# Moving convolution sums, recurrence tails and the maxima's split in a two-block network kernel

## The reference, cut to what matters

```python
def mlstm_chunkwise(q, k, v, ig, lf, state):
    ...
        inter = b + m[..., None]
        m_t = jnp.maximum(inter, jnp.max(logw, axis=-1))
        w_inter = jnp.exp(inter - m_t)
        s = jnp.einsum('bhtd,bhsd->bhts', qc, kc) * jnp.exp(logw - m_t[..., None])
        num = jnp.einsum('bhts,bhsd->bhtd', s, vc) + w_inter[..., None] * jnp.einsum('bhvk,bhtk->bhtv', C, qc)
        den = jnp.sum(s, axis=-1) + w_inter * jnp.einsum('bhk,bhtk->bht', n, qc)
        h = num / jnp.maximum(jnp.abs(den), jnp.exp(-m_t))[..., None]
...
def conv_mixer(z, w, b, ln_w, ln_b, rows):
    a = z[..., :W_C] * jax.nn.sigmoid(z[..., W_C:])
    ...
    return jax.nn.silu(layer_norm(a, ln_w, ln_b))
...
def s5_mixer(...):
    ...
        sl = s5_scan(bul.at[:, 0].add(a_bar * h0), a_bar)
    ...
        y = jnp.real(jnp.einsum('gpn,btgn->btgp', c_mat, states)) + d_mat * u
        y = jax.nn.gelu(y.reshape(u.shape[0], u.shape[1], W_D))
        return (y * jax.nn.sigmoid(y @ glu_w.astype(jnp.float32) + glu_b.astype(jnp.float32))).astype(dtype)
```

## Time and profile before

| | us |
|---|---|
| median of 3 runs (2582.73 to 2586.81) | 2583.0 |
| profiled execution | 2585.3 |
| its span | 2583.5 |
| TensorE matmuls busy | 2358.6 (91%) |
| TensorE weight loads busy | 1758.6 (68%) |
| DVE busy | 1269.9 (49%) |
| ACT busy | 769.0 (30%) |

### The profile page before, as it was taken

One profiled execution on the slowest core, in us unless ns is written; L12 is line 12 of the kernel. 1 busy time (PEld: TensorE's weight loads), 2 busy tenths in 40 slices (PEclk: granted clock), 3 DMA queues, 4 the chain that ended last, 5 costly groups with the idle time before them and its releaser, 6 DMA issues. The chain is left out here.

```text
span 2583.5 us, 26237 instructions
## 1 busy us (share of the span) xinstructions
PE 2358.6 (91%) x10746; PEld 1758.6 (68%) x10746; DVE 1269.9 (49%) x1870; ACT 769.0 (30%) x1173; POOL 141.2 (5%) x128
## 2 busy tenths in 40 slices
PE   7999897878899999999999899978797998886999
PEld 3444663667688878788878588955577876443787
DVE  3769628275554334344433464147554385553410
ACT  3100122413333322244322432334352331343310
POOL 0000000200000000000000000045100000011000
PEclk9999899659999999999999999989898998898999
DMA  7440028005233333234333221000202111001332
GB/s 251 156 129 25 1 66 334 1 1 163 74 98 97 94 97 101 80 94 131 94 94 98 74 58 42 17 1 33 78 25 82 42 41 65 5 14 46 106 98 57
DMA packets 272911, 204.15 MB, mean 79 GB/s; under 512 B 17650, under 2 KB 252458, under 8 KB 271864
## 3 DMA queue, kind: packets, MB, share of 16 engines
q1 hardware_dynamic: 257772, 186.31, 23.7%
q0 software_dynamic: 3136, 10.25, 1.1%
q10 hardware_dynamic: 11884, 5.91, 0.8%
HBM read 175.26 MB, written 26.01 MB: 78 GB/s over the span
## 5 line engine op out<-in xcount | busy, mean ns | idle before, releaser
L1919 PE MATMUL bk_in<-h_part,w_part 128*128 128x512 f32 x2112 | 485.0, 392 | 9.5 <-DVE h_part L2207 6.7
L1919 PEld LDWEIGHTS bk_in<-h_part,w_part 128*128 128x128 f32 x2112 | 398.3, 189 | 95.5 <-DVE h_part L2207 7.1
L2005 ACT ACTIVATE w_part<-w_raw 128x1024 fp32r<-128x1024 f32 (+1 forms) x136 | 154.4, 1136 | 549.4 <-PE bk_in L1919 315.9
L2142 DVE TENSOR_TENSOR w_part<-w_raw,w_part 128x1024 fp32r<-128x1024 f32 (+1 forms) x136 | 179.2, 1318 | 226.9 <-ACT w_part L2005 226.8
L1919 PE MATMUL bk_out<-hid_part,w_part 128*128 128x512 f32 x1056 | 244.5, 394 | 7.6 <-DVE hid_part L2218 7.6
L1919 PEld LDWEIGHTS bk_out<-hid_part,w_part 128*128 128x128 f32 x1056 | 201.0, 190 | 51.0 <-DVE hid_part L2218 8.4
L3618 PE MATMUL fo_ps<-fo_hi,fo_part 128*128 128x512 f32 x512 | 161.8, 395 | 21.0 <-DVE fo_part L2366 21.0
L985 PE MATMUL fr_ps<-arena,work 128*128 128x512 f32 x384 | 168.5, 600 | 5.1 <-DMA work<-in_w_in 5.1
L2479 PE MATMUL bk_in<-h_part,sj_part 128*128 128x512 f32 x576 | 135.4, 396 | 6.8 <-DVE h_part L2230 5.7
L985 PEld LDWEIGHTS fr_ps<-arena,work 128*128 128x128 f32 x384 | 73.5, 193 | 96.4 <-issue 91.2
L2889 PE MATMUL aj_ps<-h_part,aj_part 128*128 128x512 f32 x576 | 137.8, 400 | 0.0
(11 more groups left out here) (558 smaller groups left out, 3344.7 us busy)
## 6 DMA issues: line engine op xcount, KB each, us to landing
w_raw<-in_w_ffn_in SPq DMA_DIRECT2D x88, 512.0 KB, 3.8
work<-in_w_mod SPq DMA_DIRECT2D x24, 1024.0 KB, 8.0
w_raw<-in_w_ffn_out SPq DMA_DIRECT2D x32, 704.0 KB, 4.6
work<-in_w_in SPq DMA_DIRECT2D x25, 512.0 KB, 3.8
w_raw<-in_w_in SPq DMA_DIRECT2D x20, 512.0 KB, 3.8
w_raw<-in_w_out SPq DMA_DIRECT2D x16, 512.0 KB, 4.1
work<-in_w_out SPq DMA_DIRECT2D x8, 1024.0 KB, 6.9
kept_mix<-work SPq DMA_DIRECT2D x12, 512.0 KB, 2.6
```

The lines of the kernel that those rows point to most:

```text
L1919: mm = pe.matmul(bank, w_part[:, n % 2, a, k, :], moving(b, k), start=(first and k == 0 and j == 0), stop=(last and k == kt - 1 and j == 2))
L2005: nc.scalar.activation(w_part[:, n % 2, 0, 0:kt, :], w_raw[:, n % 2, 0:kt, :], ACT.Copy)\
L2142: nc.vector.tensor_tensor(w_part[:, n % 2, 1, 0:kt, :], w_raw[:, n % 2, 0:kt, :], f32(w_part[:, n % 2, 0, 0:kt, :]), ALU.subtract).then_in ...
```

## The change

In the front, `turn_inputs` comes before tile 6, `conv_sums` after job 6 and `conv_squares` after job 11; ACT takes the squares after job 9, the roots after job 12 and the gating root after job 14. The matrix `Km` (before: `K`) is brought back from HBM by SP at the end of this stage.

In the recurrence, `inputs(n + 4)` comes ahead of `modulation(n)`; modulations 14 and 15 stand behind `outputs(0)` and `outputs(1)`, and the last row turn behind the transposes, which go into four banks of `pv`. The coefficients `ca` are loaded before piece 11. DVE clears a region of 8 x 512 columns, and ACT and DVE split the maxima there, on 8 partitions; the other 120 stay zero.

In the matrix memory, `rows` contracts over all 128 partitions of this region. ACT multiplies `pE` by `w_in` (`inter`, 8 pieces of 65 columns with a scale for each partition), between its squares and roots; `norm` runs later, and the last `divide` before `gated(0)`. Buffers of the recurrence move to other addresses.

```diff
@@ -490,19 +490,16 @@
   order = [NT, NT + 1] + list(range(NT))
-  m_part = rounded(nc, S, "m_part", X0, 2, 2, T)
-  pick = rounded(nc, S, "pick8", X0 + 4 * T, 8)
+  m_part, pick = S.first_half[:, 0], S.first_half[:, 1, 0, 0:8]
   sq = A.view(X0 + 4 * T + 16, 8, HD)
...
   rs = A.view(X0 + 5 * T + 16, NT // 2, 8)
-  f32 = lambda v: v.bitcast(F32)
-
   def heads(r):
...
   with memory(S) as ctx:
-    s = semaphores(nc, S, ctx, "ml", "kt ktc vs st stc m_hi m_lo pick rows dd m0 m1 scores w ahead states intra inter sum dve"
+    s = semaphores(nc, S, ctx, "ml", "kt ktc vs st stc rows dd m0 m1 scores w ahead states intra inter scaled sum dve"
                     " centered squared var root normed turned")
@@ -515,12 +512,10 @@
           n = 4 * d + h
-          pe.wait_ge(s.pick, 1)
-          pe.wait_ge(s.m_lo, d + 1)
           for c in range(2):
             for j in range(2):
-              mm = pe.matmul(pR[:, 2 * (u % 2) + c, :], pick[0:8, n:n + 1].broadcast_to([8, P]),
-                     m_part[0:8, d, j, c * HALF:(c + 1) * HALF], start=(j == 0), stop=(j == 1))
+              mm = pe.matmul(pR[:, 2 * (u % 2) + c, :], pick[:, n:n + 1].broadcast_to([P, P]),
+                     m_part[:, 4 * d + 2 * j + c, :], start=(j == 0), stop=(j == 1))
           mm.then_inc(s.rows, 1)
@@ -529,14 +524,14 @@
           else:
-            pe.wait_ge(s.sum, 2 * i - 1)
+            pe.wait_ge(s.scaled, i)
           for a in range(2):
...
           if i:
-            pe.wait_ge(s.sum, 2 * i)
+            pe.wait_ge(s.sum, i)
           for d in range(2):
@@ -628,10 +623,6 @@
 
-        for d in range(2):
-          nc.scalar.activation(m_part[0:8, d, 0, :], S.M[d][:, :], ACT.Copy).then_inc(s.m_hi, 1)
-          if d == 0:
-            nc.scalar.activation(pick[0:8, :], S.ident[0:8, 0:8], ACT.Copy).then_inc(s.pick, 1)
         act.wait_ge(s.st, 1)
@@ -645,19 +636,34 @@
                       ACT.Exp, bias=S.a[:, i, 4 * d + h:4 * d + h + 1]).then_inc(s.dd, 1)
-        for r in range(NT // 2):
+        def inter(i):
+          act.wait_ge(s.inter, i + 1)
+          w = S.w_in[:, i, :, :, :].rearrange("p e a d -> p e (a d)")
+          for e in range(2):
+            for n in range(4):
+              at = (4 * e + n) * V1
+              o = nc.scalar.activation(sums[:, i, at:at + V1], pE[:, e, n * V1:(n + 1) * V1], ACT.Copy,
+                          scale=w[:, e, n:n + 1])
+          o.then_inc(s.scaled, 1)
+
+        def squares(r):
           act.wait_ge(s.centered, r + 1)
           nc.scalar.activation(sq, heads(r), ACT.Square).then_inc(s.squared, 1)
+
+        def root(r):
           act.wait_ge(s.var, r + 1)
           nc.scalar.activation(rs[:, r, :], rs[:, r, :], ACT.Sqrt).then_inc(s.root, 1)
+
+        for i in range(NT):
+          inter(i)
+          if i >= 2:
+            (squares if i % 2 == 0 else root)((i - 2) // 2)
+        squares(NT // 2 - 1)
+        root(NT // 2 - 1)
 
...
         step = Chain(dve, s.dve)
-        for d in range(2):
-          dve.wait_ge(s.m_hi, d + 1)
-          nc.vector.tensor_tensor(m_part[0:8, d, 1, :], S.M[d][:, :], f32(m_part[0:8, d, 0, :]), ALU.subtract)\
-            .then_inc(s.m_lo, 1)
         for r in range(4):
@@ -682,13 +688,8 @@
         def combine(i):
-          dve.wait_ge(s.inter, i + 1)
-          v = sums[:, i, :].rearrange("p (e n v) -> p e n v", e=2, v=V1)
-          nc.vector.tensor_tensor(v, pE[:, :, 0:4 * V1].rearrange("p e (n v) -> p e n v", v=V1),
-                      S.w_in[:, i, :, :, :].rearrange("p e a d -> p e (a d)").unsqueeze(3)
-                      .broadcast_to([P, 2, 4, V1]), ALU.mult).then_inc(s.sum, 1)
+          dve.wait_ge(s.scaled, i + 1)
           dve.wait_ge(s.intra, i + 1)
-          dve.wait_ge(s.sum, 2 * i + 1)
           v = sums[:, i, :].rearrange("p (e n) -> p e n", e=2)
@@ -697,7 +698,7 @@
           d8 = den[:, 16 * r:16 * r + 16]
-          dve.wait_ge(s.sum, 4 * r + 4)
+          dve.wait_ge(s.sum, 2 * r + 2)
           step(nc.vector.scalar_tensor_tensor(out=d8, in0=o[:, :, HD], scalar=-1.0, in1=o[:, :, HD],
@@ -747,14 +748,16 @@
             combine(i - 1)
+          if i >= 4 and i % 2 == 0:
+            norm(i // 2 - 2)
           if i >= 2 and i % 2 == 0:
...
             variance(i // 2 - 1)
-            norm(i // 2 - 1)
+        norm(NT // 2 - 2)
         combine(NT - 1)
+        divide(NT // 2 - 1)
         gated(0)
-        divide(NT // 2 - 1)
         variance(NT // 2 - 1)
@@ -807,8 +810,9 @@
   V.wv0 = A.view(V.w_back + 2176, 2, KT * P)
-  V.yc = A.view(WR0 + 2 * T, S5L, W_MIX)
-  V.ys = A.view(C0, 2, T)
+  V.Km = A.view(V.w_back + 2176 + 2048, S5G, P)
+  V.yc = A.view(V.w_back + 2176, S5L, W_MIX)
+  V.ys = A.view(V.w_back, 2, T)
   return V
@@ -966,8 +970,9 @@
                   S.kept_u[:, m, j, :].rearrange("(g p) c -> p g c", p=S5P)).then_inc(s.ut, 16)
+        sp.dma_start(V.Km.rearrange("p g n -> p (g n)"), S.spill[:, V.N_CA + 4 * T:]).then_inc(s.wv0, 16)
         sp.wait_ge(s.ut, 16 * 2 * S5L)
-        sp.wait_ge(s.wv0, 16)
+        sp.wait_ge(s.wv0, 32)
 
@@ -1130,17 +1135,16 @@
         tile(5)
-        tile(6)
         turn_inputs()
-        for n in range(7, Z_TILES):
+        for n in range(6, Z_TILES):
           tile(n)
...
           job(n)
-          if n == 1:
-            conv_sums()
           if n == 3:
             turn_gating_weights()
-          if n == 5:
+          if n == 6:
+            conv_sums()
+          if n == 11:
             conv_squares()
@@ -1210,17 +1214,17 @@
           o.then_inc(s.free, 1)
-          if n == 3:
+          if n == 9:
             for h in range(2):
...
                   .then_inc(c.squared, 1)
-          if n == 7:
+          if n == 12:
             for h in range(2):
...
               nc.scalar.activation(rs[:, cut[h]], rs[:, cut[h]], ACT.Sqrt).then_inc(c.inverse, 1)
-          if n == 10:
+          if n == 14:
             act.wait_ge(g.root, 1)
@@ -1574,7 +1578,7 @@
   wvT = [v.rearrange("p r (t n) -> p r t n", n=P) for v in (V.wv0, wv1)]
-  K = A.view(V.w_back + 2176 + 2048, S5G, P)
+  K = V.Km
   g = [A.view(Z0 + 10 * T + 512 + i * 2 * NS, 2, NS) for i in range(2)]
@@ -1585,12 +1589,14 @@
   gw = A.view(H0 + 7 * T + 16, 2, W_MIX)
-  sig = A.view(WR0, 2, T)
+  sig = A.view(V.ca_back, 2, T)
+  M_parts = S.first_half[:, 0]
+  f32 = lambda v: v.bitcast(F32)
   w_mod = I["w_mod"].rearrange("l (k p) n -> p (l k) n", p=P)
...
   with memory(S) as ctx:
-    s = semaphores(nc, S, ctx, "s6", "back back2 gw dve v read out gelu turned2 ys table glu sig")
+    s = semaphores(nc, S, ctx, "s6", "back back2 gw dve v read out gelu turned2 ys table glu sig zeros m_hi m_lo")
     m = semaphores(nc, S, ctx, "mo", "w0 w1 w2 done rowc turned dve zero pick")
@@ -1612,9 +1618,7 @@
           load(n)
-          if n == 8:
-            sp.dma_start(K.rearrange("p g n -> p (g n)"), S.spill[:, V.N_CA + 4 * T:]).then_inc(s.back2, 16)
-          if n == 11:
+          if n == 10:
             sp.dma_start(A.view(V.ca_back, V.N_CA), S.spill[:, 0:V.N_CA]).then_inc(s.back2, 16)
@@ -1662,12 +1666,11 @@
         pe.wait_ge(m.pick, 3)
-        for n in range(DT):
-          modulation(n)
+        for n in range(DT - 2):
           if n + 4 < DT:
             inputs(n + 4)
-        turn_row(N_MOD - 1)
-        pe.wait_ge(s.back2, 32)
+          modulation(n)
+        pe.wait_ge(s.back2, 16)
         pe.wait_ge(s.table, 1)
@@ -1690,16 +1693,18 @@
           for b in range(2):
-            if c:
-              pe.wait_ge(s.ys, b + 1)
             for j in range(4):
-              t = pe.transpose(pu[:, b, j * P:(j + 1) * P], V.yc[:, 4 * b + j, c * P:(c + 1) * P], S.ident)
+              t = pe.transpose(pv[:, 2 * c + b, j * P:(j + 1) * P], V.yc[:, 4 * b + j, c * P:(c + 1) * P],
+                      S.ident)
             t.then_inc(s.turned2, 1)
...
         outputs(0)
+        modulation(DT - 2)
         outputs(1)
+        modulation(DT - 1)
         turn_outputs(0)
         turn_outputs(1)
+        turn_row(N_MOD - 1)
         pe.wait_ge(s.gw, 16)
@@ -1715,13 +1720,21 @@
           nc.scalar.activation(pick[part, :], S.ident[part, part], ACT.Copy).then_inc(m.pick, 1)
-        for q in range(N_MOD):
+        def take_rows(q):
           act.wait_ge(m.done, 2 * q + 2)
...
             nc.scalar.activation(rows[q % 2][part, :], pu[part, q % 2, :], ACT.Copy).then_inc(m.rowc, 1)
+
+        for q in range(N_MOD - 1):
+          take_rows(q)
+        act.wait_ge(s.zeros, 2)
+        for d in range(2):
+          nc.scalar.activation(M_parts[0:8, 4 * d:4 * d + 2, :],
+                    S.M[d].rearrange("p (a b) -> p a b", b=HALF), ACT.Copy).then_inc(s.m_hi, 1)
+        nc.scalar.activation(S.first_half[0:8, 1, 0, 0:8], S.ident[0:8, 0:8], ACT.Copy)
         for half in range(2):
@@ -1730,6 +1743,7 @@
               ACT.Gelu_apprx_tanh).then_inc(s.gelu, 1)
+        take_rows(N_MOD - 1)
         for n in range(4):
@@ -1777,6 +1791,20 @@
 
+        dve.wait_ge(s.table, 1)
```

(19 more changed lines are left out.)

## The result

The changed kernel takes 2560.9 us, the median of 4 runs (2560.47 to 2561.35), against 2584.9 us for the kernel before in the same session (4 runs, 2582.73 to 2588.02). The ratio is 0.9906, with a 95% interval of 0.9889 to 0.9923. The profiled execution has a span of 2558.7 us, where that of before had 2583.5: 24.8 us less.

What follows compares the result with a forecast made beforehand. TensorE was taken as the bound, with DVE-caused gaps in the front and a 0.50 clock in the matrix memory. 5.5 + 4.2 + 9.6 = 19.3 us; 2585.3 - 19.3 - 2.3 = 2563.7 us, range 2551 to 2576 us.

Steps and rivals of the forecast that it cites:

- rival (b): Matrix memory chunks: the clock stays full and DVE bounds them, 6.5 us gained instead of 1.0; 2558.2 us, chance 0.12.
- Front, 5.5 forecast: Front: the reordering closes both convolution gaps and the gate sums come earlier; gain 5.5 us (2 to 9).
- The gap of `turn_inputs`: Front: TensorE stands still from 147.7 to 153.0 us, 5.3 us, as the transposes need DVE copies.
- Its low clock: Front: low clock expected after the 5.3 us gap, taken at 3 us with 0 and 5 as bounds.
- their 6.1 us wait: Front: TensorE reaches the gate sums at 322.1 and waits 6.1 us for DVE; low clock then loses some 0.7.
- Recurrence, 4.2 forecast: Recurrence: outputs start 8.7 us earlier, gating products at 467.4 instead of 471.6 us; gain 4.2 us (2 to 6).
- Matrix memory, 9.6 forecast: Matrix memory: 3.4 at the start, 4.5 row loop, 1.0 chunks, 0.7 end; 9.6 us (5 to 17).
- The central step: Matrix memory row loop: 128 partitions bring 2.4 GHz and ACT then bounds the rounds; 4.5 us (0 to 5).
- The end: Matrix memory's end: `divide` before `gated(0)` hides 0.70 us of waiting for the squares.
- (a): Row loop: row products stay at 0.50, padding counts no more than 8 partitions; 4.5 us less gained, 2568.2 us, chance 0.22.
- (c): Front and recurrence moves cancel, only the matrix memory's 9.6 us are left; 2573.4 us, chance 0.11.
- (d): Front: low clock from the `turn_inputs` gap holds through tiles 6 to 11, making it slower; 2593.7 us, chance 0.05.

Runs made afterwards that it cites:

- front_old: Changed kernel with the old order of the front on TensorE and ACT, Km still at the front's end: 2566.5 us, ratio 0.9924.
- sq8: Changed kernel with conv_squares after job 8 instead of 11 and ACT's squares and roots moved earlier: 2551.1 us, ratio 0.9867.
- rows8: Changed kernel with the row products contracting over 8 partitions instead of 128: 2565.1 us, ratio 0.992.
- rows64: Changed kernel with the row products contracting over 64 partitions instead of 128: 2565.5 us, ratio 0.9922.
- mod_old: Changed kernel with modulation products 14 and 15 back in front of the outputs, inputs still ahead of modulation: 2564.2 us, ratio 0.9918.
- dve_mul: Changed kernel with the multiplication by w_in back on DVE, one operation of 520 columns a chunk: 2565.1 us, ratio 0.9919.
- warm: Changed kernel with 17 overwritten row products of 512 columns filling TensorE's waits ahead of the chunks: 2555.4 us, ratio 0.9886.
- both_fill: As `both`, with six more overwritten row products ahead of the state products in chunks 3 to 6: 2538.8 us, ratio 0.9822.
- both: Changed kernel with turn_inputs behind tile 6, gating_norm in DVE's wait for the squares, and the fill of `warm`: 2540.6 us, ratio 0.9828.

## Why the prediction was right, and where its steps were off

The forecast was 2563.7 us and the kernel took 2560.9; the sum of 19.3 us met 24.8 in the span (2583.5 to 2558.7). All three parts went the way that was forecast, and all three gave more. The time looks nearer than the sum was: the forecast starts from 2583.0 us, and the kernel before had 2584.9 in the session of the result, so 24.0 us by the medians stand against 19.3. And 2560.9 lies midway between the forecast and rival (b), 2558.2 us; it is the traces that tell the two apart, not the time.

**Front, 5.5 forecast, 6.6 measured** (5.8 for the order alone, by `front_old`). The gap of `turn_inputs` was 5.51 us for 5.3. Its low clock was forecast at 3 us, from the sums behind the old gap; it took 0.6 net: from the old start of the jobs, 234.40, to 240.51 are 6.1 us. (The transposes took 1.1 us more, and the waits for DVE's copies between them shrank.) The error is that the price of a low clock was carried over from one gap to another: the window behind this gap is at 0.57, but only 3.6 us of work fell into it, and from 157 us on the clock was 1.00 again.

```profile
153.00:157.00 4.00, 3.61 (x16) 2.91 (x16) 2.87 (x6) 0.00 (x0) 0.00 (x0) 0.57 0.02 5
```

The other way round at the gate sums: 0.7 us was forecast for the low clock behind their 6.1 us wait (6.07 measured), and it took 2.9 against the trace of before, which was partly low there too. The squares came 2.9 us earlier than forecast, 2.2 of it because the jobs did. So the two clock terms missed by 2.4 and 2.2 us, in opposite directions, and nearly cancelled: that the front's sum came out so near is partly luck. The late centring and squares were seen as the next thing to be late, but not that three jobs' shift would repair it: `sq8` gives 10 us for it. `Km` landed 5.8 us after its issue at 372.7, ahead of the stage's end, and cost nothing, as forecast.

**Recurrence, 4.2 forecast, 4.9 measured.** The outputs started 14.1 - 6.6 = 7.5 us earlier relative to the stage, where 8.7 were forecast (a row turn of 1.05 us stands between product 13 and the outputs and was left out; so they began 1.9 us behind DVE's last operation, not within 1), and the way from there to the gating products took 21.7 us, where 23.5 were. The trace of before had its first outputs at half clock (L1686 took 1.86 and 1.50 us for 16 products, and 1.16 us further on), which makes 1.5 of the 1.8 us, and the way from the outputs was taken from it without seeing that. The new operations of DVE and ACT were covered: the memset took 3.47 us (bound 4.8), the two subtractions 2.35, and the next operation of DVE had 13.04 us to wait for the transposes:

```profile
437.52 3.47 DVE L1795 MEMSET h_part<- 128x4096 f32 x1 [0.92 <-DVE work L1787]
...
457.53 2.48 DVE L1806 COPY work<-s_v 128x512 f32<-128x512 f32 x4 [13.04 <-PE s_v L1697]
```

**Matrix memory, 9.6 forecast, 11.6 measured.** By the marks: to the first chunk states 3.97 us (3.4 forecast), from there to the first `out` 5.24 (4.5), the chunks 0.80 (1.0), the end 1.54 (0.7). The central step, that 128 partitions bring the full clock and ACT then bounds the loop, is shown by `rows8` and `rows64`: 4.0 us. The other 1.2 of the 5.24 come without the padding, as the loop now begins at full clock. ACT's eight pieces took 1.76 us a chunk, between the bounds of 1.7 and 2.2, and were covered.

The end is right in its reason and lucky in its size. `mod_old` has this order with the last product at half clock, as before, and takes 8.39 us from its end to the last transposes, where the kernel before took 8.99: `divide` ahead of `gated(0)` hides 0.6 us, for the 0.7 forecast. In the changed kernel the last product takes 2.07 us in place of 3.67, because the clock rises as it begins, which the prediction did not see:

```profile
542.00:544.00 2.00, 2.00 (x18) 1.89 (x16) 0.03 (x1) 1.86 (x9) 0.00 (x0) 0.97 0.00 0
```

Not all of these 1.6 us arrive. `norm` now stands before the last `combine`, and its root stands on ACT behind the eight pieces of the last chunk (`inter(7)`), so DVE waits 2.11 us for it, and `combine` starts 0.8 us after the product:

```profile
543.97 0.20 DVE L726 RECIPROCAL work<-work 128x8 f32<-128x8 f32 x1 [2.11 <-ACT work L655]
...
544.81 0.69 DVE L694 TENSOR_TENSOR work<-work,ml_o 128x520 f32<-128x520 f32 x1
```

From the end of the last product to the last transposes are 9.06 us: what the order hides, this wait takes back. The end's 1.5 us are 0.6 of the order and 0.9 of the clock, and the latter is missing in `mod_old` and `dve_mul`.

**The rivals.** (a), the row products at 0.50, did not happen; its price of 4.5 us was near the 4.0 measured. (b), the full clock through the chunks, did not happen in the changed kernel either: the clock was down when they began. Where `warm` and `both_fill` force it in part, it brings 7.0 us and 1.5 more, with DVE as the bound as the rival had it (4.90 us of 5). (c) fell: both parts kept their gains. (d) fell: tiles 6 to 11 took 82.56 us for 192 instructions, 0.43 us each, the full speed.

## What to carry to other kernels

When a group of products moves to close a gap, follow the engine that consumes it to its next rendezvous: here the squares closed one gap and opened another of 6 us with a low clock behind, and three jobs' shift was worth more than the whole reordering. A producer moved ahead of a busy engine only moves the gap to where TensorE waits for it; undo each such move alone once the rest is in place. Price a low clock from how much TensorE work stands behind the gap, not from another gap, and try filling the wait itself. Where the clock changes is not the same in every trace of the same code (1 to 1.5 us here), so a difference of that size from one trace is not yet a gain.

## What the runs showed of the hardware

- The clock of TensorE was at 0.50 through the whole row loop with 8 or 64 partitions and TensorE busy 5.00 us of 5, and at 1.00 with 128 partitions, 120 of them zeros, at 3.80 of 5. In the chunks, 128-partition products of 65 columns with 64-partition ones between them stayed at 0.50 at 5.00 of 5 in the changed kernel, and with the six wider products a chunk they ran at 1.00. What quantity the chip follows, these runs don't tell.
- The wider operand costs nothing: four row products take 1.19 us at full clock with 8 partitions as with 128.
- Waits of 2.75 us (`warm`), 2.76 (`both`) and 0.97 us (`both_fill`) in chunk 3 were each followed by a fall of the clock within 2 us, and the waits of 0.56 us in each round of the row loop were not. In the gate sums of `both`, products of 4 to 32 columns, the clock fell with no wait at all (TensorE busy 1.00 of 1 at 0.50).
